# The ring of weight blocks moves to the end of SBUF, and every other tile 28 KB lower

## What is computed

```python
def hybrid_mixer(u, w_in, ...):
    proj = u @ w_in
    ...
    y_a = (b_a * causal_dwconv(c_a * v_a, conv_a_w)) @ w_a_out
    ...
    y = ssd_chunked_scan(xh, dt, a, bs, cs)
    y_s = gated_group_rmsnorm(y, z, ssd_norm_w) @ w_s_out
    merged = jax.nn.sigmoid(gate_a) * y_a + jax.nn.sigmoid(gate_s) * y_s
    return merged @ w_o

def conv_gated_mlp(v, w_up, ffn_conv_w, ffn_conv_b, w_down):
    h1, h3 = jnp.split(v @ w_up, 2, axis=-1)
    return (jax.nn.silu(causal_dwconv(h1, ffn_conv_w) + ffn_conv_b) * h3) @ w_down

def second_block(...):
    proj = jnp.einsum('bsd,de->bse', _rmsnorm(x, norm_w), w_in)
    ...
    merged = sigmoid(ma_raw) * (y_a @ w_proj_a) + sigmoid(mb_raw) * (y_b @ w_proj_b)
    x = x + merged @ w_out
    return _rmsnorm(x, final_norm_w)
```

## The kernel before

| tile | before |
|---|---|
| raw and w_low, w_high | 16.1-32.1, 32.1-44.1 |
| X, ya_low | 44.1-60.1 |
| u_high, u_low (y_low is over both) | 60.1-76.1, 76.1-92.1 |
| par, cst, masks, tok, ws_t, sums | 92.1-107.5 |
| f_high, f_low | 107.5-151.5, 151.5-195.5 |
| a_high, m_high, b_high, n_high_rows | 123.5-139.5 |
| a_low, m_low, b_low, n_low_rows, ya_high | 139.5-155.5 |
| y_high | 155.5-187.5 |
| AG | 155.5-171.5 |
| early_high, early_low | 171.5-187.5, 187.5-203.5 |
| v_tok, Btok, k_tok, vt | 197.5, 203.5, 207.5, 213.6 and up |
| last tile ends | 223.6 |

## Time and profile before

### The profile page before, as it was taken

One profiled execution on the slowest core, in us unless ns is written; L12 is line 12 of the kernel. 1 busy time (PEld: TensorE's weight loads), 2 busy tenths in 40 slices (PEclk: granted clock), 3 DMA queues, 4 the chain that ended last, 5 costly groups with the idle time before them and its releaser, 6 DMA issues.

```text
span 1745.9 us, 22162 instructions
## 1 busy us (share of the span) xinstructions
PE 1726.6 (99%) x8792; PEld 1402.8 (80%) x8792; DVE 1149.2 (66%) x1686; ACT 816.3 (47%) x1162; POOL 27.5 (2%) x51
## 2 busy tenths in 40 slices
PE   8999999999999999999999999999999999999997
PEld 6888888878877888888888888788888888888886
DVE  6754346878876545677774446767768777767564
ACT  5323224765756323322222334667667666655521
POOL 0000000000000000000000000100000000000000
PEclk9999999999999999999999999999999999999999
DMA  4323222433332222222222333722222222222322
GB/s 165 127 98 123 87 97 96 121 97 108 120 98 73 98 95 97 96 97 96 97 97 97 108 97 108 251 78 82 81 77 73 77 74 81 73 85 73 132 95 75
DMA packets 48360, 174.76 MB, mean 100 GB/s; under 512 B 5489, under 2 KB 5617, under 8 KB 47617
## 3 DMA queue, kind: packets, MB, share of 16 engines
q1 hardware_dynamic: 43648, 155.45, 26.8%
q0 software_dynamic: 4608, 17.89, 3.1%
HBM read 164.87 MB, written 4.26 MB: 97 GB/s over the span
## 4 chain that ended last, share of the span: by engine, by line
PE 97%; DVE 1%; DMA 1%; ACT 0%; issue 0%; SPq 0%; DVEq 0%; ACTq 0%
PE bank L505 86%; PE bank L524 2%; PE bank L728 2%; PE bank L656 1%; PE bank L566 1%; PE bank L738 1%; PE bank L654 1%; DMA raw<-stream 1%; PE bank L614 1%; PE bank L774 0%; PE bank L763 0%; PE bank L751 0%; PE bank L635 0%; DVE X L2047 0%; PE bank L549 0%; DMA par<-params 0%
## 5 line engine op out<-in xcount | busy, mean ns | idle before, releaser
L505 PE MATMUL bank<-u_high,w_high 128*128 128x512 f32 x1568 | 621.4, 396 | 0.0
L505 PE MATMUL bank<-u_high,w_low 128*128 128x512 f32 x1568 | 611.0, 390 | 0.0
L505 PE MATMUL bank<-u_low,w_high 128*128 128x512 f32 x1568 | 610.9, 390 | 0.0
L839 ACT ACTIVATE w_high<-raw 128x1024 fp32r<-128x1024 f32 x285 | 301.0, 1057 | 602.0 <-PE bank L505 587.8
L1382 DVE TENSOR_TENSOR w_low<-raw,w_high 128x1024 fp32r<-128x1024 f32 x285 | 348.2, 1223 | 259.3 <-ACT w_high L839 253.6
L505 PEld LDWEIGHTS bank<-u_high,w_high 128*128 128x128 f32 x1568 | 294.4, 188 | 62.8 <-issue 3.2
L505 PEld LDWEIGHTS bank<-u_high,w_low 128*128 128x128 f32 x1568 | 294.4, 188 | 62.6
L505 PEld LDWEIGHTS bank<-u_low,w_high 128*128 128x128 f32 x1568 | 294.7, 188 | 59.3 <-issue 1.0
L1461 DVE TENSOR_TENSOR h_raw<-bank,rs 128x512 f32<-128x512 f32 x44 | 30.4, 691 | 62.2 <-PE bank L505 55.3
L505 PE MATMUL bank<-f_high,w_low 128*128 128x512 f32 x176 | 69.5, 395 | 0.0
L505 PE MATMUL bank<-f_high,w_high 128*128 128x512 f32 x176 | 69.5, 395 | 0.0
(11 more groups left out here) (357 smaller groups left out, 2437.1 us busy)
## 6 DMA issues: line engine op xcount, KB each, us to landing
raw<-stream SPq DMA_DIRECT2D x285, 512.0 KB, 3.3
rows<-running POOLq DMA_DIRECT2D x32, 256.0 KB, 3.4
X<-x_t SPq DMA_DIRECT2D x4, 512.0 KB, 7.8
u_high<-n_high_rows POOLq DMA_DIRECT2D x2, 1024.0 KB, 9.2
u_low<-n_low_rows POOLq DMA_DIRECT2D x2, 1024.0 KB, 11.5
residual<-X POOLq DMA_DIRECT2D x4, 512.0 KB, 7.4
X<-residual POOLq DMA_DIRECT2D x4, 512.0 KB, 5.4
out_t<-X SPq DMA_DIRECT2D x4, 512.0 KB, 3.6
```

The source lines that it names most:

```text
L505: ins = pe.matmul(acc[:], w[:, k], x[:, at + k], start=start and k == first and j == 0, stop=stop and k == KT - 1 and j == 2)
L839: act.activation(w_high[:, n % HI_RING], raw[:, n % RAW_RING], ACT.Copy).then_inc(hi_done, 1)
```

## The change

`raw` and `w_high` are no longer the first tiles but are placed so that the ring ends where SBUF ends, `ring_at` = (229368 - 28672) rounded down to a multiple of 64 = 200640. The tiles allocated one after the other now begin with `X` at 16512, so each of them, and with `F` all the others, lies 28672 bytes lower. (The words that came with the change say 44 KB.) The ring goes from 16.1-44.1 to 195.9-223.9 KB. Instructions, their order, semaphores and sizes are the same; only addresses differ.

```diff
-        ring_at = base[0]
-        raw = fixed("raw", [P, RAW_RING, KT, P], F32)
+
+        ring_at = (nc.sbuf_usable_end - (RAW_RING + HI_RING) * KT * P * 4) // 64 * 64
+        raw = place("raw", [P, RAW_RING, KT, P], F32, ring_at)
         w_low = place("w_low", [P, RAW_RING, KT, P], F32R, ring_at)
-        w_high = fixed("w_high", [P, HI_RING, KT, P], F32R)
+        w_high = place("w_high", [P, HI_RING, KT, P], F32R, ring_at + RAW_RING * KT * P * 4)
...
-        assert zone[0] <= nc.sbuf_usable_end and F + 116 * K <= nc.sbuf_usable_end, (zone[0], nc.sbuf_usable_end)
+        assert zone[0] <= ring_at and F + 116 * K <= ring_at, (zone[0], ring_at)
```

## The result

Median before 1747.15 us (1745.35 to 1747.69), after 1771.79 us (1771.11 to 1772.78): ratio 1.014, 95% interval 1.0127 to 1.0152. The profiled execution of after took 1772.78 us with a span of 1771.0 us, 25.1 more than the span of before. The forecast was 1744.4 us. One execution of all that follow, of e7, stands far off the others, at 1992.37 us; the ratio of e7 leaves it out.

What follows compares the result with a forecast made beforehand. TensorE's step at line 505 was taken to bound the kernel. From 1746.6 us, 2.2 us came off for tiles crossing the edge, all other terms set at nothing: 1744.4 us, range 1736 to 1775 us.

Steps and rivals of the forecast that it cites:

- The bound: Line 505, the matmul of the weight blocks on TensorE: 86% of the chain; faster copies or loads worth nothing in steady stretches.
- the map: Line 505: moving tiles up to 92 KB step at 226.6 ns, from 107.5 KB on at 232.3 to 233.3; chance 0.46.
- the DMA landings: Bulk moves at 1096.4 us: landings 10% slower from the new ring start would cost 1 us; set at nothing.
- The gain on f and the others: High tiles of f, a, m, b, n crossing the edge: 140 triples at 16 ns, 2.2 us gained, 0.8 to 5.8.
- Weights far up: nothing: Line 505 with its weights at the end of SBUF: taken as nothing; upper bound 5.7 to 6.7 ns a matmul.
- the step of u moves at all: Sign that the prediction is wrong: 4704 of 6576 matmuls hang on u's step, forecast to stay at 226.6 ns.
- The rival that the ring's place decides: Every u block: short step only with weights low or near the moving tile; 28 us slower, 1774.6 us; chance 0.31.
- The rivals that all steps become short: Line 505: long steps need data much higher than weights, so all become short; 9.9 us gained, 1736.7 us; chance 0.15.
- nothing changes: Line 505: the levels belong to something other than the offset; time stays at 1746.6 us; chance 0.08.
- The fragile step: u after a break of small matmuls: steps of 231 ns, falling to 227 after some ten; read for the ring's-place rival.
- The page of the Trainium skill: Two independent PE read ports and no term for a tile's offset: no effect of the change, 1746.6 us.

Runs made afterwards that it cites:

- e7: Kernel before with everything from F on 128 bytes higher, all tiles at phase 0; 1739.30 beside 1747.75 us, ratio 0.9953.
- e5: No kernel computation: 16 data by 16 weight starts, 32 bytes apart; phase is data start minus weight start modulo 256; steps 226.7 to 234.4 ns.
- e6: Changed kernel with the ring 320 bytes lower, at 200320; 1748.02 beside 1747.75 us, ratio 1.0001.
- e1: No kernel computation: 13 data by 13 weight places, 16 KB apart, 45 matmuls a pair; all pairs but the first step at 226.7 ns.
- e11: Changed kernel with the ring at 200576 and everything from F on 128 bytes higher; 1738.88 beside 1747.57 us, ratio 0.9953.
- e3: No kernel computation: matmul triples at the kernels' offsets, with constant values, random values, or random values beside traffic; u 226.7 ns before, 233.3 after.
- e12: No kernel computation: 8 by 8 starts at 512, 384, 256 and 128 columns, and plain float32; 256 columns 113.3 to 120.0 ns, 128 columns 111.7.
- e9: Kernel before with everything behind the ring 128 bytes higher, the ring unmoved; 1767.50 us, ratio 1.0117.

## Why the prediction was wrong

**The bound was right.** TensorE's step at line 505 sets the time; loads, copies and the splitting of weights carried 0.3 us of the difference, at the one wait for a landing.

**The step that failed is the map.** From the earlier trace rows the prediction took that low moving tiles step short and high ones long, with an edge between 92 and 107.5 KB. The numbers were right, and that offsets make the levels was right too. But before the change every tile below 107.5 KB had phase 0 and every one above it phase 128, so place and phase were the same column of the table, and the trace of one layout couldn't tell them apart. What the runs showed in its place: the phase decides, 226.7 ns at 0 and 228.9 to 234.4 elsewhere (e5), 320 bytes on the ring take back the whole loss (e6), and place moves nothing (e1, e11). The prediction had the remainders in hand: it says that the new ring starts at an odd multiple of 64 bytes and the old one at a multiple of 128. It priced that on the DMA landings alone, at 1 us (their median stays at 3.3 us, and the one wait on them grew by 0.3), and not on the matmul, whose two operands it governs. The offsets set out modulo 64, 128 and 256 beside their steps would have shown a second explanation at once.

**The gain on f and the others.** Its term was 2.2 us, from 0.8 to 5.8, for tiles crossing the edge. By the steps 5.4 us came, near the upper end, but by the phase: all k of f fell to 229.0 ns, where the prediction had its later k stay at 233.

**"Weights far up: nothing".** This term failed by size, at 0 for about +27 us. It rested on equal durations of weight loads. They are still 188 ns at a step of 233.3, so the duration of a load doesn't show what a pair of operands costs. The bound on the upper side, 5.7 to 6.7 ns on each u matmul, held the 6.7 that came. That such a bound stood there, and that "the step of u moves at all" was named as what would make the prediction wrong, is why its range to 1775 us held the time. As to the cause that is luck: the width of the range came from the price of the next rival.

**The rival that the ring's place decides.** At 1774.6 us it is 2.8 us from the result, with the right tiles (all u blocks) and nearly the right price. Its mechanism is false: e1 has weights and data up to some 200 KB apart at 226.7 ns, and in e11 the ring at the end costs nothing. It came near because the change moved place and phase together again. It also had y rise by 4.2 ns, where 1.5 came, and no gain on f. The rivals that all steps become short, or that nothing changes, fell with the step of u.

**The fragile step.** The prediction read the slow start of u after a break as for that rival. It doesn't speak for it. In e11, with the ring at the end, u after the same break takes 11 steps in 2.54 us as before, and 226 or 227 ns from there on:

```profile
406.11 0.39 PE L506 MATMUL bank<-u_low,w_high 128*128 128x512 f32 x1
...
408.65 0.39 PE L506 MATMUL bank<-u_high,w_high 128*128 128x512 f32 x1
```

So the slow start is there at phase 0 wherever the ring lies. Why it takes some ten matmuls stays open.

**The page of the Trainium skill.** SBUF — State Buffer, section Who interferes with whom, says that PE reads its moving operand and its weights over two independent ports and that "PE and ACT never wait on anyone". On the time of TensorE itself e5 doesn't bear out that the two are independent: the same instruction, with no other engine at work once the tiles are filled, takes from 226.7 to 234.4 ns by the difference of its two operands' starts. The measurement decides. On waiting for other engines e3 agrees: its columns with traffic show no level that the other columns don't have at the same phase. What in the chip repeats every 256 bytes no run here shows.

## What to carry to other kernels

When a change of layout moves tiles, write every operand's start modulo 256 beside the step of its matmuls, before and after; none of the places tried in SBUF moved it. For fp32r matmuls of 512 columns let data and weights start at the same remainder modulo 256 (33 us of 1772 lie between after and e11, for 128 bytes of padding and another rounding), and don't round to 64 bytes what depends on it. Take a step from first and last starts: the durations of pipelined matmuls and of weight loads hide or only hint at it. And before trusting a map drawn from one layout, ask what else differs between its two sides.

## What was not expected of the hardware

- The step of an fp32r matmul of 512 columns depends on the difference of the two starts modulo 256 bytes, at 226.7 to 234.4 ns, and not on either start by itself (e5, e12). Where tiles of different phases alternate it isn't the mean of theirs (ya: 228.9 ns before, where the mean is 231.1, and 231.2 in e9, where it is 228.9).
- The pattern is another one for each width: 384 columns 173.3 to 176.7 ns, 256 columns 113.3 to 120.0 and not the same for all pairs of a phase, 128 columns 111.7 at all phases. Plain float32 showed none (e12).
- Some pairs have two stable levels at the same offsets, as phase 128 with 232.4 and 233.3, or after's a with 228.9 and 233.3 in e3. Which one a stretch takes stays open.
- Behind an idle TensorE the granted clock stood at its 1.2 GHz level for the first matmuls, some 430 ns each instead of 227 (e3); the kernel itself has TensorE busy for 99% of its span and 0.995 granted, and after a wait of 9.85 us for a landing block it shows the same level once for 3.4 us (after, from 1125.0 us).
